# Channel-major projections of a decoder layer: rounded and remaining activations as one product of 512 contiguous columns

## What is computed

```python
h = rmsnorm(x, ln1_g[l])
z = h @ w_in[l]                       # one projection, 2048 x 5944, feeds both head groups
...
y_a = nsa_mixer(q, kc, vc, ks, vs, kw, vw, gl, ...)       # sparse attention
y_b = rwkv7_mixer(z_rwkv, ...)                            # a recurrence over the tokens
x = x + jnp.concatenate([rmsnorm(y_a), y_b], axis=-1) @ w_out[l]
x = x + memory_attention(rmsnorm(x), rmsnorm(mem), wq, wk, wv, wo)   # k = m @ wk, v = m @ wv
x = x + hier_moe(rmsnorm(x), ...)
return rmsnorm(x, lnf_g)
```

## Time and profile before

| | before |
|---|---|
| median of 3 runs | 1515.1 us |
| profiled execution: its own time | 1517.84 us |
| profiled execution: span | 1516.0 us |
| TensorE busy | 1451.8 us (96%) |
| VectorE busy | 731.1 us (48%) |
| ScalarE busy | 511.1 us (34%) |
| mean granted TensorE clock | 0.982 of full |

### The profile page before, as it was taken

How to read it: one execution, slowest core, us unless ns; L and a number is a source line. 1 busy time by engine, 2 the same in 40 slices (tenths; PEclk the granted TensorE clock), 3 DMA queues, 4 the chain that set the end, 5 groups by cost and what they waited for, 6 DMA issues and landing times.

```text
span 1516.0 us, 27556 instructions
## 1 busy us (share of the span) xinstructions
PE 1451.8 (96%) x11926; PEld 1107.7 (73%) x11926; DVE 731.1 (48%) x1287; ACT 511.1 (34%) x878; POOL 134.8 (9%) x263
## 2 busy tenths in 40 slices
PE   6999999999999999999999999999999899989997
PEld 6998998989899999998879997876333333333332
DVE  4683756749347555554454434554233233223325
ACT  5542423424346455554444334432110110101003
POOL 6010020201020000000000000011111010110100
PEclk9999999999999999999999999999999999999998
DMA  6642322424356544445655516683999999999996
GB/s 206 206 129 96 120 89 89 139 72 137 112 190 204 168 150 129 141 157 203 221 168 166 166 56 206 231 336 128 417 421 421 421 421 420 422 421 421 422 413 226
DMA packets 159615, 351.01 MB, mean 232 GB/s; under 512 B 13616, under 2 KB 111498, under 8 KB 135050
## 3 DMA queue, kind: packets, MB, share of 16 engines
q1 hardware_dynamic: 159498, 349.30, 62.4%
HBM read 347.18 MB, written 2.10 MB: 230 GB/s over the span
## 4 chain that ended last, share of the span: by engine, by line
PE 87%; DMA 6%; DVE 3%; issue 2%; ACT 1%; SPq 0%; DVEq 0%; ACTq 0%
PE banks L853 23%; PE banks L1377 13%; PE banks L1217 11%; PE banks L848 8%; PE banks L1237 6%; PE banks L1411 6%; DMA expert_unit<-in_moe_w_down_dram 5%; PE banks L1453 3%; PE banks L1005 1%; PE banks L1349 1%; PE banks L1262 1%; PE banks L1285 1%; DVE hidden_lo_chunks L2021 1%; PE banks L988 1%; PE banks L1180 1%
## 5 line engine op out<-in xcount | busy, mean ns | idle before, releaser
L1377 PE MATMUL banks<-expert_unit,pair_entries 128*64 128x512 f32 x1024 | 244.5, 623 | 23.1 <-issue 23.1
L853 PE MATMUL banks<-hidden_lo_chunks,piece 128*128 128x256 f32 x928 | 264.5, 285 | 0.0
L1617 ACT CAST piece<-arena_fixed 128x1024 fp32r<-128x1024 f32 (+1 forms) x160 | 164.0, 1036 | 190.4 <-PE banks L853 154.9
L2041 DVE TENSOR_TENSOR piece<-arena_fixed,piece 128x1024 fp32r<-128x1024 f32 (+1 forms) x160 | 190.5, 1213 | 59.0 <-ACT piece L1617 58.5
L1377 PEld LDWEIGHTS banks<-expert_unit,pair_entries 128*64 128x64 f32 x1024 | 74.0, 142 | 165.5 <-issue 165.5
L853 PE MATMUL banks<-hidden_hi_high_chunks,piece 128*128 128x256 f32 x928 | 181.5, 294 | 2.7 <-DVE piece L2041 2.2
L853 PE MATMUL banks<-hidden_hi_low_chunks,piece 128*128 128x256 f32 x928 | 180.9, 293 | 0.2 <-DVE piece L2041 0.2
L853 PEld LDWEIGHTS banks<-hidden_lo_chunks,piece 128*128 128x128 f32 x928 | 179.7, 194 | 0.0
L2303 DVE TENSOR_TENSOR loop_split<-arena_fixed,loop_split 128x2048 fp32r<-128x2048 f32 x48 | 107.9, 2289 | 109.3 <-ACT loop_split L1783 109.3
L853 PEld LDWEIGHTS banks<-hidden_hi_high_chunks,piece 128*128 128x128 f32 x928 | 146.2, 194 | 12.0 <-issue 8.3
L2559 DVE TENSOR_TENSOR arena_phases<-arena_phases,banks 128x512 f32<-128x512 f32 x128 | 81.8, 681 | 143.9 <-PE banks L1453 143.9
(11 more groups left out here) (405 smaller groups left out, 2086.9 us busy)
## 6 DMA issues: line engine op xcount, KB each, us to landing
expert_unit<-in_moe_w_gate_dram SPq DMA_DIRECT2D x64, 1024.0 KB, 22.9
expert_unit<-in_moe_w_up_dram SPq DMA_DIRECT2D x64, 1024.0 KB, 25.1
expert_unit<-in_moe_w_down_dram SPq DMA_DIRECT2D x56, 1024.0 KB, 22.9
arena_fixed<-in_w_in_dram SPq DMA_DIRECT2D x23, 2048.0 KB, 8.7
arena_fixed<-in_wk_mem_dram SPq DMA_DIRECT2D x8, 2048.0 KB, 9.0
arena_fixed<-in_wv_mem_dram SPq DMA_DIRECT2D x8, 2048.0 KB, 8.1
arena_fixed<-in_w_out_dram SPq DMA_DIRECT2D x8, 2048.0 KB, 8.0
arena_fixed<-in_wq_mem_dram SPq DMA_DIRECT2D x8, 2048.0 KB, 8.0
```

What stands on the lines that cost most here:

```text
L853: mm = pe.matmul(b[:, half * T:half * T + T], w(w_)[:, k % 8, :], hidden_x(x_, c), start=c + t == 0, stop=c == NC - 1 and t == 2)
L1377: mm = pe.matmul(bank[b][o, :].rearrange("p (g n) -> p g n", g=2), hs_pair[:, c, o], gate_up_unit(i(e))[:, :, c % (NC // 2), :], start=c = ...
L1617: nc.scalar.copy(piece_half(p, 0), raw_piece(p)).then_inc(piece_hi, 1)
L2041: V.tensor_tensor(piece_half(p, 1), raw_piece(p), piece_half(p, 0).bitcast(F32), ALU.subtract)\
```

## The change

The activations' hi and lo parts of a chunk now lie side by side, so that a channel-major product is two matmuls: one of 512 columns, weight hi by (activation hi, activation lo), and one of 256 columns, weight lo by activation hi. The 512 columns fill a whole bank: its first half holds hi-hi plus the weight-lo pass, its second half the activation-lo pass. So a unit of 256 output channels is now two *parts* of 16 products with a bank each, 69 parts in all (58 of them split so), which alternate between the same two banks. ScalarE copies a part's first half into its place, and VectorE adds the second half from the bank onto it.

```diff
-        hid_hi = (over("hidden_hi_low_chunks", concat_at, 8, T), over("hidden_hi_high_chunks", HI, 8, T))
-        hid_lo = over("hidden_lo_chunks", hT_at, NC, T)
+        act_chunks = (over("hidden_low_chunks", hT_at, 8, 2, T), over("hidden_high_chunks", HI, 8, 2, T))
...
+        parts = [(n, h) for n, k in enumerate(keys) for h in range(1 if k in narrow else 2)]
+        split_parts = [(n, h) for n, h in parts if keys[n] not in narrow]
+
+        def part_bank(n, h=0):
+            return parts.index((n, h)) % 2
+
+        def part_begin(i):
+            n, h = parts[i]
+            return 2 * NC * n + NC * h
...
+        def part_out(n, h=0):
+            return act_proj.at(keys[n]) if keys[n] in narrow else halves_added(n, h)
...
-                b = bank[n % 2]
-                if r == 0 and n >= 2:
-                    pe.wait_ge(*act_proj.at(keys[n - 2]))
+                half = r // NC if key not in narrow else 0
+                b = bank[part_bank(n, half)]
+                if r == NC * half:
+                    i = parts.index((n, half))
+                    if i >= 2:
+                        pe.wait_ge(*part_out(*parts[i - 2]))
...
-                    half, c = divmod(r, NC)
-                    for t, (x_, w_) in enumerate(PASSES):
-                        mm = pe.matmul(b[:, half * T:half * T + T], w(w_)[:, k % 8, :], hidden_x(x_, c),
-                                       start=c + t == 0, stop=c == NC - 1 and t == 2)
+                    c = r % NC
+                    pe.matmul(b[:, :], w(0)[:, k % 8, :], act_chunks[c // 8][:, c % 8].rearrange("p a t -> p (a t)"),
+                              start=c == 0, stop=False)
+                    mm = pe.matmul(b[:, 0:T], w(1)[:, k % 8, :], hidden_x(0, c), start=False, stop=c == NC - 1)
...
-                    if p % 4 == 3:
-                        copy_out(p // 4)
+                    copy_out(p)
...
+            def add_halves(until):
+
+                for n, h in split_parts[added[0]:until]:
+                    dve.wait_ge(first_half, split_parts.index((n, h)) + 1)
+                    o = projection_into(keys[n], h)
+                    V.tensor_tensor(o, o, bank[part_bank(n, h)][:, T:2 * T], ALU.add).then_inc(added_half, 1)
+                added[0] = max(added[0], until)
...
+            def add_before(old, new):
+
+                ended = [i for i in range(len(parts)) if part_begin(i) + 2 * NC // (1 + (keys[parts[i][0]] not in narrow)) <= old]
+                wanted = [i - 2 for i in range(2, len(parts)) if part_begin(i) < new]
+                add_halves(max(halves_of(len(ended)), halves_of(max(wanted, default=-1) + 1)))
...
-                passed[0] = filling.step()[1] // 8
+                old, new = filling.step()
+                add_before(old, new)
+                passed[0] = new // 8
...
+                mix(2).then_inc(*dve_rw.mark(("mix", g)))
                 gap()
-                mix(2).then_inc(*dve_rw.mark(("mix", g)))
```

More of the change, by code:

```diff
@@ new lines, in copy_out @@
+                if key not in narrow:
+                    if i % 2:
+                        act.wait_ge(piece_read, p + 1)
+                        if key[0] == "rkv":
+                            act.wait_ge(*(dve_rw.at(("mix", key[1] - 1)) if key[1] else dve_c.at("mixm")))
+                        nc.scalar.copy(projection_into(key, i // 2), bank[part_bank(n, i // 2)][:, 0:T]).then_inc(first_half, 1)
+                    return
+                if i < 3:
+                    return
+                act.wait_ge(piece_read, 4 * n + 4)
@@ L1580, in copy_out @@
+                b = part_bank(n)
+                if key == "misc2":
+                    nc.scalar.copy(zraw[0:32, 3, 1:T + 1], bank[b][0:32, 0:T])
+                    ins = A(gate_rows[32:56, :], bank[b][32:56, 0:T], ACT.Tanh, scale=0.5)
+                elif key[0] == "mv":
+                    ins = nc.scalar.copy(vm[:, :, key[1] * UC:key[1] * UC + UC], b2(b))
+                else:
+                    ins = nc.scalar.copy(vsw[:, ("vs", "vw").index(key[0])], b2(b))
                 ins.then_inc(*act_proj.mark(key))
@@ L2042, in piece_rest, with halves_of @@
                     .then_inc(piece_lo, 1)
[L2044 removed]
+            filling, passed, issued, added = Filling(GAPS, 0, 32 * NW), [0], [NPW], [0]
+            def add_halves(until):
[4 more added lines that the diff above has]
+                added[0] = max(added[0], until)
+            def halves_of(count):
+                return sum(keys[n] not in narrow for n, h in parts[:count])
+            def add_before(old, new):
+                ended = [i for i in range(len(parts)) if part_begin(i) + 2 * NC // (1 + (keys[parts[i][0]] not in narrow)) <= old]
+                wanted = [i - 2 for i in range(2, len(parts)) if part_begin(i) < new]
+                add_halves(max(halves_of(len(ended)), halves_of(max(wanted, default=-1) + 1)))
             def gap():
```

81 lines of the change are left out of this document (43 added, 38 removed).

## The result

The changed kernel takes 1539.7 us (median of 4 runs, 1539.1 to 1540.1) where the kernel before took 1515.2 in the same comparison: ratio 1.0159, 95% interval 1.0144 to 1.0173, slower by 24 us. The forecast was 1524 in a range of 1513 to 1534: right in its direction, a third of the size. The profiled execution's span is 1538.2 us.

The account below looks back on a forecast made before the run. The prediction took TensorE to bound the kernel. Its terms, -11.4 + 8.8 + 7.15 + 4.2 = +8.8 us, gave 1526.6 us on the profiled execution and 1524 us on the median's scale, range 1513 to 1534.

Parts of the forecast that it names:

- What TensorE saves: All 928 products: each goes from 359.7 to 347.4 ns, saving 12.3 ns, in all -11.4 us.
- The opening stage: Heads of units 1, 3 and 4: TensorE waits for an add behind a remainder, 2.98, 2.97 and 2.88 us, +8.8 together.
- The recurrence: Recurrence: added work delays steps TensorE waits for: `kn` +1.05, `bon` of group 1 +2.8, `tI` +0.8, other places +2.5; +7.15 us.
- Elsewhere it is one add of 0.42 against a margin: Six other places in the recurrence: a 0.42 us add delays each step, less small margins plus the shortened gap, +2.5 us.
- The memory stage: Memory stage: 256 products save 3.1 us, and its adds cost nothing because no step is within 1 us of TensorE.
- The clock: Behind four new waits of 2.8 us or more: three falls of the granted clock at 1.4 us each, +4.2 us.
- VectorE falls behind through the recurrence: Rival, recurrence and memory stage: adds delay remainders, delays don't heal, a piece comes late; 1535 us, chance 0.07.
- Nothing is saved on TensorE: Rival, all products: a 512-column matmul costs as much as two of 256; +20.2 us, 1535, chance 0.04.
- The waits come, the clock holds: Rival: waits without clock falls, or half the recurrence's waits swallowed; +4.6 us, 1519.7, chance 0.30.
- The rule of bank turns: Rival, all split parts: the clock falls at most bank turns, 81 us more, near 1600, chance 0.01.
- The pair that is cheaper than its parts: Rival, all products: the wide matmul hides both fixed parts, 320 ns a product, -37 us, 1498, chance 0.08.
- The 131 ns for 512 columns: Rival, all products: loads and matmuls overlap at that spacing, 96 ns less each, 89 us, near 1435, chance 0.01.

Follow-up runs that it names:

- changed kernel's two ratios: The changed kernel against the kernel before, measured twice with nothing altered: 1.0159, then 1.0150 in a repeat that also gave a second profile.
- no adds: The changed kernel without VectorE's 58 adds, the second half of each bank computed but never read: ratio 0.9954 to the kernel before.
- adds first: The changed kernel with VectorE's adds ahead of the remainders whose buffers came free later: 1517.8 us, ratio 1.0013 to the kernel before.
- opening as changed: The changed kernel with adds ahead of the remainders only in the recurrence and memory stage, opening stage left in the changed kernel's order: ratio 1.0099.
- grouped order: On top of adds first, each run of products of one piece does all 512-column matmuls, then all 256-column ones: ratio 1.0013 to the kernel before.
- Filling the idleness: The changed kernel with 36, 22 and 18 unused matmuls on TensorE ahead of the waits at units 1, 3 and 4: ratio 1.0117.
- narrow matmuls with the adds first: The adds first kernel with three 256-column matmuls again for each product but the first of each part: ratio 1.0039 to the kernel before.
- best version of the new matmuls: Wide matmuls only in opening units 0 and 2 to 4 and the memory keys, grouped, copies and adds first; rest narrow: 1513.7 us, ratio 0.9984.

## Why the prediction was wrong

The runs divide the change in their own terms. The measured column adds up to 1.0155, the mean of the changed kernel's two ratios, by the way it is made: each row is the difference of two neighbouring versions. So the sum proves nothing, and each row is good to 2 to 3 us.

| part | predicted | measured | from |
|---|---|---|---|
| the matmuls' form | -11.4 | -7.0 | no adds: 0.9954 |
| opening stage, with its falls | 8.8 + 4.2 (all falls) | 13.0 | adds first against opening as changed |
| steps of the recurrence delayed (measured: all that the adds cost in the good order) | 7.15 | 8.9 | no adds against adds first |
| adds behind remainders, 304 to 912 | none | 8.4 | opening as changed against changed |
| sum | 8.8 | 23.3 | changed kernel, mean of two: 1.0155 |

**What TensorE saves** was mis-sized. The two prices came from dense stretches of one form each and were right there (230 and 119 ns in the grouped order). In alternation a product takes 347 ns in some stretches and 353 in others. Over all dense stretches at full clock it is 351 ns, and three narrow matmuls in the kernel before are 359: a saving of 8 ns and not 12.3, 7.6 us over 928 products, which agrees with the run without adds. This term is 4.4 us of the 14.5 that are missing.

**The opening stage** was right in its mechanism and places: three waits, each for the add behind a remainder. Their lengths were 4.47, 2.78 and 2.23 us against 2.98, 2.97 and 2.88, 9.5 in sum against 8.8; that the errors nearly cancel is luck. So is the 13.0 against 8.8 + 4.2: the 4.2 were for falls behind four waits, one of them in the recurrence, and in the second profile of the changed kernel the stage ends only 8.8 us later than before, with one slow stretch as before. The first wait was longer because its end hangs on a transfer and its beginning on TensorE: the profile of before had a slow stretch in unit 0, which made TensorE late by about 1.5 us, and the prediction took the idle spot from that profile.

**The recurrence** is the step that failed. It took 8.9 us longer, with no more slow stretches in it than before, where the prediction's terms for it (-6.7 and +7.15) come to 0.5. "I went through every gap of the four groups and asked how far VectorE's releasing step ended before TensorE needed it": that asks after the steps that TensorE waited for before. The change made new ones, the first product of each part, and "Elsewhere it is one add of 0.42 against a margin" priced only how far an add pushes the old steps. In the gaps of products 304, 464, 480, 624 and 912 the add is itself what TensorE needs next, and what stands ahead of it is not 0.42 but two or three remainders, 2.4 to 3.5 us. These five waits are 9.4 us in the trace, and with the adds ahead of the remainders only the 1.8 at products 320 and 480 stay. The term that stood at nothing measured 8.4 us, the largest part of what is missing. The same rule had been found and applied in the opening stage, and was not carried on. Of the steps that were named, `kn` waits 0.9 us in the changed kernel's trace (predicted 1.05; 0.5 of it is there without any add), `bon` of group 1 nothing in the changed kernel and 1.28 once the stall ahead of it is gone (2.8), `tI` nothing. The sum of 7.15 came out near the 8.9 that the adds cost in the good order, with other members: that is luck.

**The memory stage** "nothing" was wrong by one wait of 1.54 us at product 912, of the same kind; its saving of 3.1 us was 2.2 by the traces of the versions that have no wait there, and is eaten up in the changed kernel (240.8 us against 241.0), mostly by that wait.

**The clock.** Three falls behind four waits were forecast; of the opening stage's three waits, all had a slow stretch behind them in the first profile of the changed kernel and one in the second. The price of 1.4 us holds for a short stretch; the long one behind unit 1 cost 2.6. Filling the idleness took 5.7 us off (give or take 2.9), and no fall was left behind the three waits, so falls do follow idleness, though no one place can be counted on.

**The rivals.** "VectorE falls behind through the recurrence" gives nearly the measured time (1535), yet the runs speak against it: with the same work in another order the loss is gone. It is not load but place. "Nothing is saved on TensorE" gives 1535 as well, and the run without adds and the narrow matmuls with the adds first speak against it (7.0 and 3.9 us saved). "The waits come, the clock holds" (1519.7) lies still further from the measurement, and both profiles have falls behind waits. The rule of bank turns (the Trainium skill, "TensorE: Matmul & The Clock Gate", section "A second HAM failure mode: psum-queue depth-cycling") fares no better: the kernel without adds has the changed kernel's 69 turns and is 7.0 us faster than before, with a granted clock of 1.00, 0.99 and 1.00 in the three stages where the kernel before had 0.97, 0.99 and 1.00. By that rule it would have been slower, so the trace doesn't bear it out here.

The pair that is cheaper than its parts is ruled out: in alternation it costs 347 to 353 ns, and in the grouped order, where the parts stand alone, they cost 349 together. The 131 ns for 512 columns of the same page's section "Back-to-back issue gap" are not seen either: with nothing between them, eight such matmuls, each with its own load, stand 230 ns apart.

## What to carry to other kernels

When a result is split so that a second engine must finish it before a bank comes free, list every turn of that bank over the whole program and ask of each what stands ahead of the releasing instruction in its engine's own order; old waits show where the engine used to be needed, not where it will be. Work that somebody needs next goes ahead of work with slack of several pieces: here that order was worth 21 us, nine times what the best version of the new matmuls gained. And a form that saves 2% of a stage's matmuls pays only where the extra steps fall into idle time of the other engines, so apply it there and leave the serial stage alone.

## What the hardware did that was not expected

Alternating matmuls of 512 and 256 columns run at one of two paces under the same code, 0.347 or 0.353 us a pair, both at a granted clock of 1.00. At the slower pace the pairs take 349, 350 and 361 ns in turn. The cause is open.

A fall of the clock follows idleness in the mean but not place by place: the same waits of 2.78 and 2.23 us were followed by a granted clock of 0.52 and 0.54 in one profile and 1.00 in the next, and a slow stretch lasted 3.4 us in most places and 6.8 in some. A term for falls belongs into the range rather than into the sum.
